# One table set for logarithm and exponential, and two retention gate units placed behind the norm sum

## The chip, the cores and the metric

The kernel runs on one core of a Trainium2 chip. The metric is the device time of one execution in microseconds (us), lower is better. The core has five engines with a queue of instructions each: TensorE (PE, matrix products; its weight loads are shown as PEld), VectorE (DVE), ScalarE (ACT), GpSimd (POOL) and SyncE (SP, which only starts transfers here). They wait for each other through semaphores. ScalarE looks its non-linear functions up in a table set; where a function is not in the loaded set, an ACT_TABLE_LOAD instruction stands before it.

## The reference

Four mixer layers with a feed-forward block behind each work on 512 tokens of width 1024, all in float32. Cut to what the change touches:

```python
# first block: layer 0 latent attention (MLA), layer 1 gated linear recurrence (HGRN)
h = h + rms_norm(mixer(rms_norm(h, g0)), g1)
h = h + rms_norm(sq_relu_mlp(rms_norm(h, g2)), g3)
# HGRN, per head: log_f = log(lb + (1-lb)*sigmoid(f_x)); exp of its cumulated sums; silu(q_x); silu(g_x)
# second block: layer 0 sparse attention (DSA), layer 1 retention
x = x + mixer_2(rms_norm_2(x, g))
x = x + conv_ffn(rms_norm_2(x, g))       # (silu(a) * b) @ w_down
# retention, 4 heads, 256 key and 512 value columns each
ret = rms_norm_2(intra + cross, out_g)   # over the 512 columns of a head
y = ret * silu(g)                        # g: 512 gate columns of the head
out = y @ w_out
```

Each `rms_norm` is x * (mean(x*x) + eps) ** -0.5 * gain.

## The kernel before

**Projections.** Everything is kept transposed: 128 channels on the partitions, 512 tokens along the row. A projection is cut into units, a unit being 128 output columns. SyncE loads a slab of weights (one to four units) into one of two `raw` buffers. GpSimd splits each unit's weights into a high and a low float32r half (`w_hi`, `w_lo`, lines 1176 to 1182; `lo_split` counts finished units), and TensorE makes three products for each chunk of 128 input channels (lines 585 to 587), 24 matmuls for a unit of 8 chunks and 12 for one of 4. Weights and results have a ring of four places: GpSimd may split unit j once unit j-4 is multiplied, and TensorE may begin unit j once VectorE or ScalarE has taken the result of unit j-4 out of its bank (`bank_free`). `unit` does one unit, `units_together` runs several units side by side chunk by chunk, `unit_pair` does two units except their last chunk, then the last chunk of both. A new slab is loaded when its `raw` buffer has been split; `raw_free` gives the count of `lo_split` for which SyncE waits. For the first slab of the second feed-forward block, which runs in a loop, the count is reached when the second of the last four units of the retention's output projection is split.

**Inputs of a projection.** They are split too. ScalarE writes the high half (`a_hi`, line 650, or `g_hi`, line 568), VectorE the low half (`a_lo`, line 663, or `g_lo`, line 572).

**Norms.** ScalarE squares the chunks (line 499), VectorE adds them (line 511), TensorE sums over the partitions with a matrix of ones (line 519), and ScalarE makes the factor in `Norm.root`: a logarithm (line 473), then an exponential of -0.5 times it (line 477). The two functions are looked up in different table sets, so a load stands between them. `AddedNorm.warm` (line 504) runs a one-element logarithm early, so that the logarithm's set is there before the sum. A `LateNorm` stands ahead of a mixer or feed-forward block and is applied to its results, so that units can start before its factor is known; a `PostNorm` stands behind one, in the first block only, and its factor must be there before the residual `hT` can be updated.

**HGRN.** Eight heads. While TensorE works on head i, the gates of head i+1 are prepared on ScalarE (`hg_gates`: SiLU, sigmoid, logarithm, four exponentials) and VectorE; then come head i's norm, the SiLU of the next gate, and `hg_turned`, two copies (lines 1261 and 1263) for which TensorE waits at line 1804.

**Retention.** Four heads, three in a loop and the last one written out with stage `st_ret_end`, whose units are 0 to 3 (values), 4 to 7 (gate) and 8 to 15 (output projection, 4 chunks each). TensorE does the value units, the scores, the four gate units with the remaining scores between them, then scores times values (line 1981) and the two matmuls of the norm sum (lines 549 and 551). VectorE then multiplies each of the four blocks of 128 value columns with gain and factor (line 1680) and with the gate (line 1684), ScalarE rounds it (568) and VectorE makes the low half (572); the output units read these. The second feed-forward block follows directly.

**Keys.** The half-zeroed copies of keys that let two 64-wide heads share one product (`k_rope_odd`, `idx_keys`) are already in this kernel.

Of the kernel before, what the change touches and what calls it, by code (L numbers as in the profile page):

```python
# [182 lines left out]
def program(nc, x, positions, norm_gains, mla_w_in, mla_q_norm, mla_kv_norm, mla_w_uq, mla_w_ukv, mla_w_o, hgrn_w_in,  # L183
# [3 lines left out]
    with ExitStack() as ctx:  # L187
# [52 lines left out]
        qk_gain, act_warm = sb("qk_gain", 1), sb("act_warm", 2)  # L240
# [185 lines left out]

        class Norm:
# [54 lines left out]
        class AddedNorm(Norm):  # L482
# [3 lines left out]
            def __init__(self, chunks, total, tiles=None):  # L486
                super().__init__(chunks)
                self.total, self.running, self.tiles = total, aux[1][:], tiles or sq
# [145 lines left out]
        class LateNorm:  # L634
# [3 lines left out]
            def __init__(self, gain_name, gain_at, total, tiles=None):  # L638
                self.norm = AddedNorm(DC, total, tiles)
                self.high, self.low = shared("late_hi", DC), shared("late_lo", DC)  # L640
                self.gain = (gain_name, gain_at)
# [36 lines left out]
        class PostNorm:  # L678


            def __init__(self, gain_at, total):
                self.norm = AddedNorm(DC, total)
# [126 lines left out]
        pre_mla = LateNorm("norm", 0, tile(F, 12), sq + [tmp[0]] + [tile(F, 8 + k) for k in range(4)])  # L809
# [293 lines left out]
        pre_ret = LateNorm("mix", DC, tile(F, 14))  # L1103
# [12 lines left out]
        ret_o, ret_raw_ready, ret_y = signal("ret_o", RV), signal("ret_raw_ready", RV, credit=1), signal("ret_y", RV)  # L1116
        n_ret = PairedNorm(RET_HEADS, RET_DV, ret_vT[0])
# [70 lines left out]
        def _(act):  # L1188
# [57 lines left out]
            def hg_gates(i):  # L1246
# [4 lines left out]
                act.activation(hg_logf, hg_f, ACT.Ln).then_inc(hg_logf_ready.sem, 1)  # L1251
                act.wait_ge(*hg_d_ready.at(0, i))
# [19 lines left out]
            with act.Fori(0, HG_HEADS - 1) as i:  # L1272
# [3 lines left out]
                hg_silu(3, hg_gate, hg_gate_ready, i + 1)  # L1276
            hg_turned(HG_HEADS - 1)
# [29 lines left out]
            for r, (b, h) in enumerate(REL):  # L1307
# [7 lines left out]
                if r == IDX_HEADS - 1:  # L1315
                    n_key.root(act, users=idx_ready.at(1))
# [7 lines left out]
            act.wait_ge(*r_factors.at(1))  # L1324
            by_block = lambda t, b: t.rearrange("p (c b) -> p c b", b=TB)[:, :, b:b + 1]
# [21 lines left out]
            def ret_head(st, i, h):  # L1347
# [12 lines left out]
                for m in range(RV):  # L1360
                    s_ret.round(act, tile(g_hi, m), m, h)
            with act.Fori(0, RET_HEADS - 1) as i:
                ret_head(st_ret, i, i)
            ret_head(st_ret_end, 0, RET_HEADS - 1)
# [4 lines left out]
        def _(dve):  # L1369
# [281 lines left out]
            def ret_head(st, i, h):  # L1651
# [17 lines left out]
                take(5, ret_gate[1])  # L1669
                decay(2)  # L1670
                take(6, ret_gate[2])
                decay(3)
                take(7, ret_gate[3])
# [23 lines left out]
            with dve.Fori(0, RET_HEADS - 1) as i:  # L1697
                ret_head(st_ret, i, i)
# [339 lines left out]
```

## Time and profile before

| what | us |
|---|---|
| median of 3 runs (lowest, highest) | 2728.09 (2726.54, 2731.78) |
| profiled execution, whole | 2730.05 |
| profiled execution, first to last instruction (span) | 2728.2 |
| PE busy in it | 2608.1 (96%) |
| POOL busy | 1917.2 (70%) |
| DVE busy | 1086.0 (40%) |
| ACT busy | 729.8 (27%) |

A busy PE is modelled: a matmul of 512 columns is shown with 0.39 us, but at full clock the next one starts 0.227 us after it. The shares are averages over very different stages, so the stages have to be looked at one by one.

### The profile page before, as it was taken

To read this page: it belongs to the slowest core of one execution; us is meant where nothing else is said; L and a number is where in the kernel's file an instruction comes from. 1 tells how busy PE (TensorE), PEld (TensorE's weight loads), DVE (VectorE), ACT (ScalarE), POOL (GpSimd) and SP (SyncE) were. 2 spreads that over 40 slices of the span, in tenths; PEclk is the share of its full clock that TensorE was granted. 3 is DMA by queue.
4 is the path that set the end of the run, shared out by engine and by line. 5 is a ranking of instruction groups with operands and counts; after the bars stand their busy time and mean duration, and the time that the engine had idled before them with its cause. 6 is when DMAs were issued, how large, how long until landed. Compare 5 with 4: busy or idle time off the path is not lost.

```text
span 2728.2 us, 33032 instructions
## 1 busy us (share of the span) xinstructions
PE 2608.1 (96%) x11887; PEld 2113.0 (77%) x11887; DVE 1086.0 (40%) x1898; ACT 729.8 (27%) x1181; POOL 1917.2 (70%) x1652
## 2 busy tenths in 40 slices
PE   6998999998998799999898999999999999899999
PEld 5776888876887688888666888888777877688887
DVE  6443211126766241112457452525441441452433
ACT  3443111014555231001455331202122021321211
POOL 5455888886665578888532588887967856788785
PEclk9999999999999899999899999999999999899999
DMA  4121223332221123233210133332312222233232
GB/s 150 51 70 62 93 93 101 99 92 62 63 76 62 51 83 99 92 97 103 62 47 31 47 107 94 93 95 91 108 62 92 77 66 73 78 107 94 93 97 73
DMA packets 285698, 224.27 MB, mean 82 GB/s; under 512 B 14387, under 2 KB 278556, under 8 KB 285468
## 3 DMA queue, kind: packets, MB, share of 16 engines
q1 hardware_dynamic: 285020, 222.47, 26.6%
q8 instruction: 69, 1.13, 0.2%
q10 hardware_dynamic: 576, 0.40, 0.1%
q14 instruction: 33, 0.27, 0.0%
HBM read 220.75 MB, written 2.10 MB: 82 GB/s over the span
## 4 chain that ended last, share of the span: by engine, by line
PE 86%; DVE 6%; issue 3%; ACT 2%; POOL 1%; DVEq 1%; DMA 1%; ACTq 0%; SPq 0%; POOLq 0%
PE proj L585 26%; PE proj L587 26%; PE proj L586 26%; PE aux L1981 1%; DVE top L1599 1%; PE aux L1823 1%; DVEq L1602 1%; PE aux L1958 1%; POOL w_lo L1182 1%; PE aux L452 1%; PE proj L746 1%; PE aux L519 0%; PE aux L805 0%; POOL w_hi L1177 0%; ACT L477 0%
## 5 line engine op out<-in xcount | busy, mean ns | idle before, releaser
L585 PE MATMUL proj<-a_hi,w_hi 128*128 128x512 f32 x2096 | 836.7, 399 | 37.8 <-DVE a_lo L663 30.3
L587 PE MATMUL proj<-a_hi,w_lo 128*128 128x512 f32 x2096 | 821.7, 392 | 0.0
L586 PE MATMUL proj<-a_lo,w_hi 128*128 128x512 f32 x2096 | 821.5, 392 | 0.0
L1176 POOL TENSOR_TENSOR w_hi<-raw,small 128x512 fp32r<-128x512 f32 x374 | 391.8, 1047 | 576.4 <-PE proj L587 552.6
L1177 POOL TENSOR_TENSOR w_hi<-raw,small 128x512 fp32r<-128x512 f32 (+2 forms) x450 | 484.7, 1077 | 177.6 <-PE proj L587 177.4
L1182 POOL TENSOR_TENSOR w_lo<-raw,w_hi 128x512 fp32r<-128x512 f32 (+2 forms) x450 | 590.5, 1312 | 6.0
L1181 POOL TENSOR_TENSOR w_lo<-raw,w_hi 128x512 fp32r<-128x512 f32 x374 | 486.8, 1302 | 29.3
L585 PEld LDWEIGHTS proj<-a_hi,w_hi 128*128 128x128 f32 x2096 | 397.6, 190 | 129.9 <-issue 39.9
L585 PE MATMUL proj<-g_hi,w_hi 128*128 128x512 f32 x1200 | 473.3, 394 | 16.0 <-DVE g_lo L572 9.9
L586 PE MATMUL proj<-g_lo,w_hi 128*128 128x512 f32 x1200 | 469.6, 391 | 0.0
L587 PE MATMUL proj<-g_hi,w_lo 128*128 128x512 f32 x1200 | 469.2, 391 | 0.0
L586 PEld LDWEIGHTS proj<-a_lo,w_hi 128*128 128x128 f32 x2096 | 397.8, 190 | 85.5 <-issue 3.9
L587 PEld LDWEIGHTS proj<-a_hi,w_lo 128*128 128x128 f32 x2096 | 397.0, 189 | 84.6
L585 PEld LDWEIGHTS proj<-g_hi,w_hi 128*128 128x128 f32 x1200 | 226.8, 189 | 68.0 <-issue 12.7
L587 PEld LDWEIGHTS proj<-g_hi,w_lo 128*128 128x128 f32 x1200 | 227.0, 189 | 47.7
L586 PEld LDWEIGHTS proj<-g_lo,w_hi 128*128 128x128 f32 x1200 | 227.1, 189 | 47.5 <-issue 1.0
L864 ACT ACTIVATE aux<-aux 128x512 f32<-128x512 f32 x64 | 37.3, 582 | 486.8 <-DVE aux L885 464.6
L1081 DVE SCALAR_TENSOR_TENSOR F<-aux,cols,F 128x511 f32<-128x511 f32 (+1 forms) x176 | 131.9, 749 | 83.1 <-ACT F L1051 73.0
L1051 ACT ACTIVATE F<-aux,cols 128x512 f32<-128x512 f32 x88 | 68.6, 779 | 225.2 <-DVE aux L1075 224.3
L1075 DVE TENSOR_TENSOR aux<-proj,F 128x512 f32<-128x512 f32 x88 | 61.5, 698 | 167.5 <-PE proj L587 138.8
L898 DVE TENSOR_TENSOR acc<-proj,acc 128x512 f32<-128x512 f32 x48 | 33.2, 692 | 210.1 <-PE proj L587 210.1
L885 DVE SCALAR_TENSOR_TENSOR aux<-proj,F 128x512 f32<-128x512 f32 x48 | 33.6, 699 | 206.4 <-PE proj L587 206.4
(272 smaller groups left out, 2192.4 us busy)
## 6 DMA issues: line engine op xcount, KB each, us to landing
raw<-in_mlp_w SPq DMA_DIRECT2D x64, 1024.0 KB, 5.3
raw<-in_f_w_up SPq DMA_DIRECT2D x88, 512.0 KB, 4.8
raw<-in_b_w_in SPq DMA_DIRECT2D x24, 1024.0 KB, 5.2
raw<-in_hgrn_w_in SPq DMA_DIRECT2D x32, 512.0 KB, 4.9
raw<-in_f_w_down SPq DMA_DIRECT2D x16, 1024.0 KB, 4.9
raw<-in_b_w_out SPq DMA_DIRECT2D x8, 1024.0 KB, 5.0
raw<-in_a_w_in SPq DMA_DIRECT2D x6, 1024.0 KB, 5.2
raw<-in_f_w_down SPq DMA_DIRECT2D x8, 768.0 KB, 4.2
```

The costliest lines, as they stand in the source:

```text
L585: pe.matmul(psum[r][:], w_hi[r][:, w], xh, start=k == 0, stop=False)
L586: pe.matmul(psum[r][:], w_hi[r][:, w], xl, start=False, stop=False)
L587: last = pe.matmul(psum[r][:], w_lo[r][:, w], xh, start=False, stop=k == kc - 1)
L864: act.activation(self.square[j % 2], self.relu[j % 2], ACT.Square).then_inc(self.split.whole.sem, 1)
L885: dve.scalar_tensor_tensor(self.relu[j % 2], bank[:], 0.0, rstd, ALU.max, ALU.mult).then_inc(*taken(self.st, j))
L1051: act.activation(u, self.x[s][j % 2], ACT.Identity, bias=conv_col(l, 3, c), scale=conv_col(l, 2, c)).then_inc(tap2.sem, 1)
L1075: dve.tensor_tensor(x, bank[:], rstd, ALU.mult).then_inc(*taken(st, n))
L1081: dve.scalar_tensor_tensor(u[:, back:T], x[:, 0:T - back], conv_col(l, k, i * DC + first + j + s * FF2C), u[:, back:T], ALU.mult, ALU.add) ...
L1176: pool.tensor_tensor(hi[:, 0:n], src[:, 0:n], nothing.to_broadcast([P, n, P]), ALU.subtract)
L1177: pool.tensor_tensor(hi[:, n:], src[:, n:], nothing.to_broadcast([P, s.kc - n, P]), ALU.subtract).then_inc(hi_split, 1)
L1181: pool.tensor_tensor(lo[:, 0:n], src[:, 0:n], hi[:, 0:n].bitcast(F32), ALU.subtract)
L1182: pool.tensor_tensor(lo[:, n:], src[:, n:], hi[:, n:].bitcast(F32), ALU.subtract).then_inc(lo_split, 1)
```

## The change

1. **Table sets.** `log_and_exp` loads the set that holds both logarithm and exponential, by name. It is called ahead of the norms that follow a SiLU or a sine (`load=True`: the first norm of the kernel, both feed-forward norms and the retention norm of the second block), in HGRN between the logarithm and the exponentials, once behind the HGRN loop, and in each retention head behind the SiLUs of its gate. All other norms go on with the set that is loaded. `warm` and its one-element logarithm are gone. Two places of DSA load the set `natural_log` by name instead.
2. **Two gate units later.** In the last retention head, gate units 6 and 7 stand behind the norm sum on TensorE; ScalarE and VectorE take them, apply SiLU and multiply between the steps of the output blocks (`ret_late_gate`). The remaining scores move ahead of unit 5. The first two output units run as a pair.
3. **Order of first units.** In both feed-forward blocks of the second block and in the retention, the first two units run one after the other, not side by side.

```diff
+        def log_and_exp(act):
+            act.preload_act_table_set("natural_log_exp_and_others")
...
             def square(self, act, src, c):
-                if c == 0 and self.tiles is sq:
-                    self.warm(act)
+                if c == 0 and self.tiles is sq and self.load:
+                    log_and_exp(act)
...
-                if c == self.chunks - 1 and self.tiles is not sq:
-                    self.warm(act)
-            def warm(self, act):
-                act.activation(act_warm[:, self.gbase % 2:self.gbase % 2 + 1], eps, ACT.Ln)
+                if c == self.chunks - 1 and self.tiles is not sq and self.load:
+                    log_and_exp(act)
...
-        pre_mla = LateNorm("norm", 0, tile(F, 12), sq + [tmp[0]] + [tile(F, 8 + k) for k in range(4)])
+        pre_mla = LateNorm("norm", 0, tile(F, 12), sq + [tmp[0]] + [tile(F, 8 + k) for k in range(4)], load=True)
...
-                self.pre = LateNorm("ffn", DC * l, tile(F, 14))
+                self.pre = LateNorm("ffn", DC * l, tile(F, 14), load=True)
...
-                            units_together(pe, st, range(2), DC, a_hi, a_lo, i, self.pre.low.at)
+                            unit(pe, st, 0, DC, a_hi, a_lo, i, ready=self.pre.low.at)
+                            unit(pe, st, 1, DC, a_hi, a_lo, i)
                             self.pre.norm.sum(pe)
...
-        pre_ret = LateNorm("mix", DC, tile(F, 14))
+        pre_ret = LateNorm("mix", DC, tile(F, 14), load=True)
...
                 act.activation(hg_logf, hg_f, ACT.Ln).then_inc(hg_logf_ready.sem, 1)
+                log_and_exp(act)
...
+            log_and_exp(act)
             hg_turned(HG_HEADS - 1)
...
                 if r == IDX_HEADS - 1:
+                    act.preload_act_table_set("natural_log")
                     n_key.root(act, users=idx_ready.at(1))
...
             act.wait_ge(*r_factors.at(1))
+            act.preload_act_table_set("natural_log")
...
-            def ret_head(st, i, h):
+            def ret_head(st, i, h, last):
...
-                for m in range(RV):
+                early = 2 if last else RV
+                for m in range(early):
                     emptied(act, st, 4 + m, i)
                     act.activation(ret_gate[m], ret_gate[m], ACT.Silu)
+                log_and_exp(act)
...
                     s_ret.round(act, tile(g_hi, m), m, h)
+                    if last and 1 <= m < RV - 1:
+                        emptied(act, st, 4 + m + 1, i)
+                        act.activation(ret_gate[m + 1], ret_gate[m + 1], ACT.Silu).then_inc(ret_late_gate.sem, 1)
...
                         dve.wait_ge(*ret_y.at(m, h))
+                        if last and m >= 2:
+                            dve.wait_ge(*ret_late_gate.at(m - 2))
                         s_ret.free(dve, m, h)
...
                         s_ret.rest(dve, tile(g_lo, m - 1), tile(g_hi, m - 1), m - 1, h)
+                    if last and 1 <= m < RV - 1:
+                        take(4 + m + 1, ret_gate[m + 1])
...
-                for m in range(RV):
+                for m in range(2 if last else RV):
                     unit(pe, st, RV + m, DC, a_hi, a_lo, i)
                     if m == 0:
                         turn(RV - 1)
-                    elif m <= 2:
+                        if last:
+                            scores(2)
+                            scores(3)
+                    elif m <= 2 and not last:
                         scores(m + 1)
...
                 n_ret.sum(pe, h)
...
+                if last:
+                    for m in range(2, RV):
+                        unit(pe, st, RV + m, DC, a_hi, a_lo, i)
...
+                if paired:
+                    unit_pair(pe, st, j, RV, g_hi, g_lo, i, lambda k: s_ret.low.at(k, h))
+                for m in range(2 if paired else 0, DC):
+                    unit(pe, st, j + m, RV, g_hi, g_lo, i,
                          ready=(lambda k: s_ret.low.at(k, h)) if m == 0 else None)
```

## Rows read from the trace of the kernel before

**Rows 1.** The page's first part: busy time, share and instructions of each engine

```profile
PE 2608.1 (96%) x11887; PEld 2113.0 (77%) x11887; DVE 1086.0 (40%) x1898; ACT 729.8 (27%) x1181; POOL 1917.2 (70%) x1652
```

**Rows 2.** Stretches: us, busy of PE, PEld, DVE, ACT, POOL, granted clock, DMA share, GB/s

```profile
960.00:1300.00 340.00, 340.00 (x1497) 281.04 (x1496) 76.00 (x115) 52.25 (x86) 281.94 (x248) 1.00 0.29 93
...
1362.00:1366.00 4.00, 4.00 (x9) 2.39 (x9) 0.00 (x0) 2.28 (x3) 2.26 (x2) 0.50 0.56 199
...
2325.00:2330.00 5.00, 4.38 (x9) 2.53 (x9) 4.20 (x7) 1.24 (x2) 0.00 (x0) 0.50 0.00 0
```

**Rows 3.** Waits of PE: us in total, times, longest us

```profile
PE proj L585 <- DVE a_lo L663: 30.3, 4, 9.3
...
PE proj L585 <- DVE g_lo L572: 9.9, 6, 7.7
...
PE proj L585 <- POOL w_lo L1182: 7.9, 3, 4.6
...
PE aux L1804 <- ACT acc L1263: 6.6, 6, 1.2
...
PE aux L452 <- ACT F L444: 3.8, 3, 2.5
```

**Rows 4.** Groups of ACT instructions: busy us, mean ns, idle time before them

```profile
L477 ACT ACT_TABLE_LOAD x28 | 35.9, 1283 | 0.5
...
L473 ACT ACT_TABLE_LOAD x16 | 20.5, 1283 | 16.2 <-PE aux L452 15.3 <-PE aux L551 0.8
```

**Rows 5.** ACT in order of time, at five places: start, us, instruction

```profile
721.84 1.28 ACT L477 ACT_TABLE_LOAD   x1
...
946.43 1.28 ACT L477 ACT_TABLE_LOAD   x1
947.72 0.63 ACT L477 ACTIVATE F<-F 128x512 f32<-128x512 f32 x1
...
1359.38 1.28 ACT L1296 ACT_TABLE_LOAD   x1
...
1456.34 1.28 ACT L1327 ACT_TABLE_LOAD   x1
```

**Rows 6.** PE in order of time, where it waited, and around the last retention head

```profile
662.14 0.38 PE L1783 MATMUL aux<-F 128*128 128x128 f32 x1 [2.90 <-DVE F L1522]
...
729.45 0.39 PE L1804 MATMUL aux<-acc 32*128 32x128 f32 x4 [1.10 <-ACT acc L1263]
...
1361.57 1.19 PE L452 MATMUL aux<-F,ones_half 128*128 128x512 f32 x1 [2.53 <-ACT F L444]
...
2315.97 1.11 PE L551 MATMUL aux<-F,ones 128*128 128x512 f32 x2
2324.74 0.76 PE L585 MATMUL proj<-g_hi,w_hi 128*128 128x512 f32 x1 [7.65 <-DVE g_lo L572]
...
2356.11 0.77 PE L585 MATMUL proj<-a_hi,w_hi 128*128 128x512 f32 x1 [4.61 <-POOL w_lo L1182]
...
2369.16 0.59 PE L519 MATMUL aux<-F,ones 128*128 128x512 f32 x1
```

**Rows 7.** DVE in order of time, behind the last retention norm

```profile
2321.12 0.75 DVE L1680 SCALAR_TENSOR_TENSOR acc<-acc,cols,F 128x512 f32<-128x512 f32 x1 [6.65 <-ACT F L477]
2321.91 0.69 DVE L1684 TENSOR_TENSOR F<-acc,F 128x512 f32<-128x512 f32 x1
```

**Rows 8.** POOL in order of time, output units 12 and 13, then the feed-forward's first

```profile
2331.70 1.04 POOL L1177 TENSOR_TENSOR w_hi<-raw,small 128x512 fp32r<-128x512 f32 x1 [22.59 <-PE proj L587]
...
2335.25 1.04 POOL L1177 TENSOR_TENSOR w_hi<-raw,small 128x512 fp32r<-128x512 f32 x1 [1.15 <-PE proj L587]
...
2345.12 1.04 POOL L1176 TENSOR_TENSOR w_hi<-raw,small 128x512 fp32r<-128x512 f32 x1 [1.68 <-DMA raw<-in_f_w_up]
...
2350.06 1.49 POOL L1176 TENSOR_TENSOR w_hi<-raw,small 128x512 fp32r<-128x512 f32 x1
```

**Rows 9.** SP in order of time: the load for the feed-forward block

```profile
2338.16 41.33 SPq L1149 DMA_DIRECT2D raw<-in_f_w_up  x10
```

More of the change, by code:

```diff
@@ L482, in program, with __init__ @@
         class AddedNorm(Norm):
[L486 removed]
+            def __init__(self, chunks, total, tiles=None, load=False):
                 super().__init__(chunks)
[L488 removed]
+                self.total, self.running, self.tiles, self.load = total, aux[1][:], tiles or sq, load
             def square(self, act, src, c):
                 n = len(self.tiles)
[L493 to L494 removed]
+                if c == 0 and self.tiles is sq and self.load:
+                    log_and_exp(act)
                 if self.base > 0 and c == 0:
@@ L634, in program, with __init__ @@
         class LateNorm:
-            def __init__(self, gain_name, gain_at, total, tiles=None):
-                self.norm = AddedNorm(DC, total, tiles)
+            def __init__(self, gain_name, gain_at, total, tiles=None, load=False):
+                self.norm = AddedNorm(DC, total, tiles, load)
                 self.high, self.low = shared("late_hi", DC), shared("late_lo", DC)
@@ L678, in program, with __init__ @@
         class PostNorm:
-            def __init__(self, gain_at, total):
-                self.norm = AddedNorm(DC, total)
+            def __init__(self, gain_at, total, load=False):
+                self.norm = AddedNorm(DC, total, load=load)
                 self.scaled, self.added = shared("post_scaled", DC), shared("post_added", DC)
@@ L1649, in ret_rotate, with ret_head @@
                     dve.tensor_tensor(dst[1], tmp[1], dst[1], ALU.add).then_inc(ret_qk_ready.sem, 1)
-            def ret_head(st, i, h):
+            def ret_head(st, i, h, last):
                 def take(j, dst):
@@ L1668, in ret_head @@
                 take(4, ret_gate[0])
[L1669 to L1673, printed above, removed]
+                if last:
+                    decay(2)
+                    decay(3)
+                    take(5, ret_gate[1])
+                else:
+                    take(5, ret_gate[1])
+                    decay(2)
+                    take(6, ret_gate[2])
+                    decay(3)
+                    take(7, ret_gate[3])
                 dve.wait_ge(*ret_v_turned.at(2, h))
@@ L1936, in _ @@
             ffn[0].pe(pe)
-            units_together(pe, st_ret_qk, range(2), DC, a_hi, a_lo, 0, pre_ret.low.at)
+            unit(pe, st_ret_qk, 0, DC, a_hi, a_lo, ready=pre_ret.low.at)
+            unit(pe, st_ret_qk, 1, DC, a_hi, a_lo)
             pre_ret.norm.sum(pe)
@@ L1942, in _, with ret_head @@
                 unit(pe, st_ret_qk, j, DC, a_hi, a_lo)
-            def ret_head(st, i, h):
+            def ret_head(st, i, h, last):
                 def turn(m):
@@ L1957, in scores @@
                     for c in range(2):
-                        last = pe.matmul(aux[b % 2][:, 0:w], ret_k[c][:, b * P:b * P + P], ret_q[c][:, b * P:T],
+                        done = pe.matmul(aux[b % 2][:, 0:w], ret_k[c][:, b * P:b * P + P], ret_q[c][:, b * P:T],
                                          start=c == 0, stop=c == 1)
-                    last.then_inc(ret_scores.sem, 1)
+                    done.then_inc(ret_scores.sem, 1)
                 for m in range(RV):
@@ L1980, in ret_head, with ret_out @@
                         e = b * RET_DV + m * P
-                        last = pe.matmul(aux[2 + m % 2][:, b * P:T], ret_vtok[:, e:e + P], ret_s[b][:, 0:T - b * P],
+                        done = pe.matmul(aux[2 + m % 2][:, b * P:T], ret_vtok[:, e:e + P], ret_s[b][:, 0:T - b * P],
                                          start=b == 0, stop=b == TB - 1, skip_group_check=True)
-                    last.then_inc(ret_o.sem, 1)
+                    done.then_inc(ret_o.sem, 1)
                 n_ret.sum(pe, h)
-            def ret_out(st, j, i, h):
-                for m in range(DC):
-                    unit(pe, st, j + m, RET_DV // P, g_hi, g_lo, i,
+                if last:
+                    for m in range(2, RV):
+                        unit(pe, st, RV + m, DC, a_hi, a_lo, i)
+            def ret_out(st, j, i, h, paired=False):
+                if paired:
+                    unit_pair(pe, st, j, RV, g_hi, g_lo, i, lambda k: s_ret.low.at(k, h))
+                for m in range(2 if paired else 0, DC):
+                    unit(pe, st, j + m, RV, g_hi, g_lo, i,
                          ready=(lambda k: s_ret.low.at(k, h)) if m == 0 else None)
             with pe.Fori(0, RET_HEADS - 1) as i:
-                ret_head(st_ret, i, i)
+                ret_head(st_ret, i, i, False)
                 for j in range(8, 12):
```

15 lines of the change are left out of this document (8 added, 7 removed).

## The prediction

> **What bounds the kernel now.** I read the page's first part, then the granted clock and busy times by stretch, the waits of TensorE, the load groups of ScalarE, and last the timeline around each wait. TensorE is busy 96% of the span [rows 1]. In a long stretch of MLP blocks it never pauses: 1497 matmuls in 340 us at full clock, so 0.227 us each, 5.45 us for a unit of 24 and 2.72 us for one of 12 [rows 2]. There nothing on another engine can gain or lose time. What is left are TensorE's waits, and their list is short: 30.3 us for the low half of an input in 4 places, 9.9 us for `g_lo` in 6, 7.9 us for split weights in 3, 6.6 us for HGRN's copies in 6, 3.8 us for a square in 3 [rows 3]. So each part of the change is worth what it takes out of one of these waits, plus what the clock does: behind some waits it is granted at 0.50, which of its two levels is 1.2 GHz [rows 2].
>
> **Part 1, the table loads.** A load takes 1.283 us. 28 stand between a norm's logarithm and exponential and 16 before the logarithm [rows 4]. Counting through the diff, 108 loads become 60, but most stand where TensorE has other work (every `LateNorm`: units run while its factor is made). Those on TensorE's path:
>
> - The four `PostNorm`s: the chain is sum, logarithm, load, exponential, update of `hT`, `a_hi`, `a_lo`, and TensorE idles all through (the 30.3 us). The logarithm's load was already early; the one before the exponential goes [rows 3, 5]: 4 x 1.28 = 5.1. Late next is the same chain without the load, so all of it counts.
> - HGRN's loop: TensorE waits 1.10 for the copies at line 1804 [rows 6], six times, 6.6 in sum [rows 3]. ScalarE reaches them by norm, rounding and gate SiLU, and the load between logarithm and exponential lies in that chain [rows 5]. Without it the copies are 1.28 earlier, a little more than the wait. The shown waits start from a modelled matmul end that lies some 0.16 behind the next possible issue (0.39 shown against 0.227). So between 6.6 and 6 x 1.28 = 7.7; I take 7.2, as wait plus overlap just fits into the load. The new load behind the gates' logarithm replaces an automatic one.
> - HGRN's entry: TensorE waits 2.90 for the first head's gates, behind the norm's factor [rows 6]; that chain loses one load: 1.3. The loads for SiLU, sigmoid and logarithm stay.
> - Short waits for `g_lo`: apart from the 7.65 [rows 6], the 9.9 holds 2.2 in five waits [rows 3]. Three of them, 1.6 together, lie in MLA and in HGRN's last head, behind norms that lose two loads or one, more than each wait: 1.6 (bounds 0 and 2.2). The extra load behind HGRN's loop comes while TensorE runs two early output units; without that cover it would cost 1.28.
> - DSA: TensorE waits 2.53 for a square that stands behind a load and a small exponential [rows 5, 6]: 1.3. Behind this wait the clock is at 0.50 for 4 us in which 9 matmuls run [rows 2], 2.0 us more than 9 x 0.227. Half the wait may or may not keep the clock up: I take half, 1.0 (bounds 0 and 2.0). Against it: the load at line 1327 started directly behind a copy [rows 5], and the named load now stands behind two semaphore waits, with the logarithms and the query copies queued behind it and TensorE waiting for those. It can be late by 0 to 1.28; I take 0.5, since VectorE's selection ends at about the same time. Sum 1.8.
>
> In the retention loop the new load stands before the first square. TensorE has scores times values, then four more units there, so I cost it at nothing; if the first copy came too late for its third group of matmuls, it would be up to 1.28 a head.
>
> **A page against the row.** The load's neighbour starts 0.01 us behind it: 946.43 plus 1.28, then 947.72 [rows 5]. The Trainium skill, "ScalarE: Activation LUTs", section "What ACT_TABLE_LOAD costs", gives 1283 ns for the load and about 1380 ns more for a drain. By it an estimate of the four `PostNorm`s would be 10.6 instead of 5.1. The drain is not in this row, so the load alone counts.
>
> **Part 3, order of first units.** With `units_together` TensorE needs two split units, now one. At the retention's start that is a short wait for weights; the 7.9 us in 3 waits [rows 3] is 4.6 at the second feed-forward (counted below) and 3.3 elsewhere, most of it in HGRN's output projection, which doesn't change. I take 0.5 (bounds 0 and 3.3). The first feed-forward starts without a wait: 0.
>
> **Part 2, the two gate units.** Clock zero is the end of the norm sum, 2315.97 + 1.11 = 2317.08 in the trace before [rows 6]. Before, the first low half lets TensorE go at 7.65, at half clock at first [rows 2]; then come 8 output units; then 4.61 of waiting for weights; and at 52.1 (2369.16) the two first feed-forward units are done [rows 6]. Their pure work is 8 x 2.72 + 2 x 5.45 = 32.7, so 19.4 us are waits and slow clock. The gate units cost 10.9 ahead of zero, so the old stretch is 63.0.
>
> After, from the same zero, which now comes 10.9 earlier:
> - Factor: 2321.12 was 4.04 behind zero [rows 7]; without two loads 1.5. First low half 3.6 later (2324.74 - 2321.12): 5.1.
> - Second: VectorE must take unit 6, done at 5.45, then 0.7 for each of take, multiply, product and low half [rows 7], SiLU 0.6 between: 8.3 to 9. ScalarE has to load the SiLU set here, but while it waits for VectorE.
> - Third and fourth: unit 7 is done at 10.9, taken at 11.7, multiply, product: 13.1, low half 13.8, last rounding and low half 14.5. These waits sit in VectorE's queue; behind them are only the output blocks, for which TensorE waits.
> - TensorE: gate units to 10.9, two chunks of unit 8 to 12.3, waits to 13.9, then 18 matmuls of the pair to 18.0, units 10 to 15 to 34.3.
> - GpSimd: before, unit 12 was begun at 2331.70, unit 13 waited 1.15, and the feed-forward load started at 2338.16, 6.46 later, 5.3 without the wait; the weights were used from 2345.12, 6.96 behind the load's start; unit 16 took 4.94, unit 17 with hand-over 6.05 [rows 6, 8, 9]. After: unit 8 is done at 17.3, unit 12 begins at 17.7, the load starts at 23.0, unit 16 is split from 30.0 to 35.0, unit 17 is ready at 41.0.
> - TensorE: unit 16 from 35.2 to 40.7 (part 3: it needn't wait for unit 17), unit 17 from 41.0 to 46.5. Its input is complete some 3 us behind 34.3, earlier than chunk 7 needs it.
>
> 63.0 - 46.5 = 16.5. Bounds: only the idle time at the norm goes, 7.65 and two small waits, 8.3; everything goes, 19.4.
>
> **Sum.** 5.1 + 7.2 + 1.3 + 1.6 + 1.8 + 0.5 + 16.5 = 34.0. The profiled execution took 2730.05, 1.96 above the median of 2728.09; by it 2696.0, by the median 2694.1. I give 2694.
>
> **The rivals.**
> - *The weights give the gain back*: GpSimd or the load for the feed-forward keeps its old time, so the output units run earlier but TensorE waits longer at 2356 [rows 6]. For it: the load starts only behind unit 13's split [rows 8, 9]. Against: unit 13 itself hangs on TensorE's unit 9, which moves. Gain 8.3 there, 25.8 in all: 2702.
> - *The named loads change nothing*: automatic loads stay wherever they were. Then parts 2 and 3 alone remain, 17.0: 2711. The trace before has two loads in each norm although one set could serve both [rows 4], so placement doesn't look for it. The Trainium skill, "ScalarE activation tables: per-element evaluation and per-set limits", section "Table sets in the compiler and the runtime", says that loads are placed by the longest run per block. By that rule the pair would have been one load already; the trace disagrees.
> - *The clock gains more*: with shorter waits it stays up behind DSA's wait and at HGRN's output too, 5 us more than I took: 2689.
> - *Slower*: the new order leaves TensorE at 0.50 from the last retention head on. Rows show 0.50 beside waits and 1.00 over the long stretch without one [rows 2], which speaks against it. Each us at half clock costs half a us of work, so it decides from 2 x 34 = 68 us; lasting 100 us it gives -34 + 50: 2744.
> - *No change* needs most of the waits to be taken over by others, such as VectorE in HGRN and GpSimd in the retention: 2727.
>
> **How the numbers follow.** Forecast 0.70 (its own range 2686 to 2702), weights 0.12, named loads 0.07, clock 0.06, no change 0.03, slower 0.02. The range reaches from the clock case with every term at its upper bound, 2684, to a point between the weights and the named loads, 2707. Within 0.2% (5.5 us) is what a measurement of this kernel can't tell from no change. Faster by more: 0.70 + 0.12 + 0.07 + 0.06 = 0.95; same 0.03; slower 0.02.
>
> **What would show it.** In the profile after: some 60 loads, none at line 477 outside DSA's two named places; the waits for `a_lo` at about 25 in 4; no wait at 1804 for the copies; two gate units directly behind the norm sum, then less than 3 us of waiting and a clock of 1.00; the wait for `w_lo` before the second feed-forward at about 1; from norm sum to that block's own sum 46.5 us. The forecast is wrong if the first low half is late because VectorE stands at a gate unit, if the feed-forward load doesn't move with unit 13, or if the copies at 1804 wait for something else than the norm.

## The result and the profile after

| | median us | lowest to highest | runs |
|---|---|---|---|
| before | 2728.11 | 2726.54 to 2731.78 | 4 |
| after | 2690.86 | 2688.88 to 2692.70 | 4 |

After takes 0.986 of before, 95% interval 0.9845 to 0.9875: faster by 37.25 us, where 34.0 were forecast. The profiled execution after took 2692.35 (span 2690.6). Its page begins with

```profile
PE 2594.2 (96%) x11887; PEld 2106.2 (78%) x11887; DVE 1090.8 (41%) x1898; ACT 666.6 (25%) x1121; POOL 1922.3 (71%) x1652
```

against [rows 1]. TensorE's idle time fell from 2728.2 - 2608.1 = 120.1 to 2690.6 - 2594.2 = 96.4, so by 23.7. The same 11887 matmuls are shown busy for 13.9 us less. That second part is the clock: a matmul at half clock is drawn longer. More than a third of the gain of the traces, 13.9 of 37.6 us, comes this way.

ScalarE's table loads, by group (the sites with one load each left out):

```profile
L429 ACT ACT_TABLE_LOAD x17 | 21.8, 1283 | 0.2
L1247 ACT ACT_TABLE_LOAD x17 | 21.8, 1283 | 0.3
L1254 ACT ACT_TABLE_LOAD x8 | 10.3, 1283 | 0.1
...
L1362 ACT ACT_TABLE_LOAD x4 | 5.1, 1283 | 0.1
```

Of the two big groups of [rows 4], 28 and 16 loads, one load is left; all sites together hold 60 loads. Line 429 is the new named load. TensorE's waits that answer to [rows 3]:

```profile
PE proj L586 <- DVE a_lo L664: 26.5, 4, 9.1
...
PE aux L1952 <- ACT F L1346: 7.3, 2, 5.2
...
PE proj L586 <- POOL w_lo L1185: 3.4, 2, 2.8
...
PE proj L586 <- DVE g_lo L573: 2.6, 1, 2.6
...
PE aux L456 <- ACT F L448: 2.6, 3, 1.2
```

The wait for HGRN's copies (6.6 in 6) is no longer in the list. `g_lo` fell from 9.9 to 2.6, the weights from 7.9 to 3.4, and the wait for a square in DSA went from 2.53 to 1.25. The second row grew, from 6.6 in 2 places; it stands in DSA and comes back below. TensorE at the end of the retention, from the norm's second sum to the sum of the second feed-forward's own norm:

```profile
2281.73 1.11 PE L552 MATMUL aux<-F,ones 128*128 128x512 f32 x2
...
2297.76 0.79 PE L586 MATMUL proj<-g_hi,w_hi 128*128 128x512 f32 x1 [2.63 <-DVE g_lo L573]
...
2320.48 0.50 PE L586 MATMUL proj<-a_hi,w_hi 128*128 128x512 f32 x1 [0.65 <-POOL w_lo L1185]
...
2331.53 1.02 PE L520 MATMUL aux<-F,ones 128*128 128x512 f32 x2
```

With the forecast's zero, the end of the norm sum at 2281.73 + 1.11 = 2282.84, the stretch is 48.7 us. Before, it was 63.0 with the gate units' 10.9 [rows 6]; the forecast was 46.5.

Two traces are compared below by the start of the same matmul in each. The start-up alone (waits for the first tables and the input) differs by about 1 us between executions of one kernel, so single differences under 1 us say little. The clock behind a wait can differ by more with the same code, as shown further below; so the table says where the time went in these two traces, and not what each step is worth in every execution.

| step of the forecast | forecast | by the two traces |
|---|---|---|
| four `PostNorm`s | 5.1 | 5.1 |
| HGRN's loop | 7.2 | 6.8 |
| HGRN's entry | 1.3 | 1.1 |
| short `g_lo` waits | 1.6 | 6.1 (MLA 1.0, HGRN's last head 3.3, its output units 1.8) |
| DSA | 1.8 | 2.9 (2.55 - 0.68 + 1.05) |
| start of the retention | 0.5 | 0.8 |
| norm sum to second feed-forward | 16.5 | 14.4 |
| start-up | 0 | 0.4 |
| sum | 34.0 | 37.6 |

### The profile page after: what moved, and what is told of

It is laid out like the page before. It is cut to its first block, busy times and chain, and to the rows that moved or that the text cites. A ratio compares the mean times of both kernels' runs of the same rounds, so it can differ in the third digit from the quotient of the medians.

```text
span 2690.6 us, 32976 instructions
## 1 busy us (share of the span) xinstructions
PE 2594.2 (96%) x11887; PEld 2106.2 (78%) x11887; DVE 1090.8 (41%) x1898; ACT 666.6 (25%) x1121; POOL 1922.3 (71%) x1652
## 4 chain that ended last, share of the span: by engine, by line
PE 92%; DVE 4%; issue 2%; ACT 1%; DMA 0%; POOL 0%; ACTq 0%; DVEq 0%; SPq 0%; POOLq 0%
PE proj L586 28%; PE proj L587 27%; PE proj L588 27%; PE aux L2006 1%; PE aux L806 1%; PE aux L1844 1%; PE aux L1980 1%; PE aux L1923 1%; PE aux L456 1%; PE proj L747 1%; PE aux L1928 1%; PE aux L520 0%; DVE F L694 0%; PE proj L1783 0%; PE proj L1784 0%
## 5 line engine op out<-in xcount | busy, mean ns | idle before, releaser
L586 PE MATMUL proj<-a_hi,w_hi 128*128 128x512 f32 x2096 | 834.5, 398 | 28.6 <-DVE a_lo L664 26.5
L865 ACT ACTIVATE aux<-aux 128x512 f32<-128x512 f32 x64 | 37.3, 582 | 489.3 <-DVE aux L886 464.6
```

The costliest lines, as they stand in the source:

```text
L586: pe.matmul(psum[r][:], w_hi[r][:, w], xh, start=k == 0, stop=False)
L865: act.activation(self.square[j % 2], self.relu[j % 2], ACT.Square).then_inc(self.split.whole.sem, 1)
```

## Experiments

### Each part alone

Part 1 alone is the kernel after with `ret_head(..., False)` everywhere, output units not paired, and `units_together` at both places. Part 2 alone has the old tables and `units_together`. Part 3 alone is:

```diff
-units_together(pe, st, range(2), DC, a_hi, a_lo, i, self.pre.low.at)
+unit(pe, st, 0, DC, a_hi, a_lo, i, ready=self.pre.low.at)
+unit(pe, st, 1, DC, a_hi, a_lo, i)
```

and the same two lines for `st_ret_qk`. Then the kernel after without part 3, and the kernel after without part 2.

Expected of part 1 alone:

> Part 1 alone on the kernel before. The forecast's terms give 5.1 (PostNorms) + 7.2 (HGRN's loop) + 1.3 (its entry) + 1.6 (short waits) + 1.8 (DSA) = 17.0, and one load less behind the retention's last norm sum, where TensorE waited 7.65 us: 1.3 to 2.6 more there, unless the weights take it back at the second feed-forward. So 2710, and 2711 if they do. If the two traces' alignment is right instead, the parts outside the retention's end are worth 23.3 us with part 3's small share in them, so 2705. If the named loads changed nothing, it would stay at 2728.

Of part 2 alone:

> Part 2 alone: the two gate units behind the norm sum, with the old table loads and with the first feed-forward units still side by side. The forecast for parts 2 and 3 together was 16.5 from the norm sum on. Side by side, TensorE can begin the pair of units only when unit 17 is split, so about 5.4 us of that should be missing: 11 us, so 2717. The factor is two loads (2.6 us) later behind the norm sum, but hidden behind the two gate units (10.9 us). If the old loads do sit on the path, 8 us, 2720. If the weights take all of it back: 0 to 3 us.

Of part 3 alone:

> Part 3 alone: first units one after the other. At the second feed-forward TensorE waited 4.61 us for two split units; it would need only unit 16 first, and unit 17 is ready about 6 us after it, while unit 16's matmuls take 5.45. So about 4 of the 4.61 us go, and up to 0.5 at the retention's start: 4.5 us, 2723.6. The rival, that the input's last chunk (not the weights) is what comes late there, gives 0.5 us or less, 2727.6, which could not be told from no change.

Of after without part 3:

> The kernel after without part 3 (first units of the second and later blocks side by side again). In the trace after, unit 17 is ready about 5.3 us behind unit 16. With both needed at the start, the forecast's reckoning makes it slower than the kernel after by 5 us, 2696. If part 3 is worth only its wait in the kernel before (4.0), 2695; if the weights were no limit after part 2, the difference is below 1 us, 2691.

Of after without part 2:

> The kernel after without part 2 (all four gate units of the last head ahead of its norm sum, output units not paired). By the runs so far, from the norm sum to the second feed-forward's own sum (10.9 us added where the gate units lie ahead of it) the tables alone took 59.5 us, tables with gates late 55.4, all three 48.7, old tables with part 3 alone 54.7. If the parts add up, this one takes 59.5 - 6.7 = 52.8, so 4.1 us more than after: 2695. If part 3 is worth more here, as it was on the old kernel (8.3), 51.2 and 2693.4. By the forecast, in which the gate units were most of 16.5 us, it would be about 10 us slower than after, 2701.

Measured (medians of 4 to 12 executions; "stretch" is the retention's end as above, from the norm sum to the feed-forward's own sum, with 10.9 added where the gate units lie ahead of the sum):

| parts | us | ratio to before, 95% | stretch | wait for weights in it |
|---|---|---|---|---|
| none (before) | 2728.1 | 1 | 63.0 | 4.61 |
| 1 | 2701.7 | 0.9906 (0.9894 to 0.9919) | 59.5 | 4.57 |
| 2 | 2721.5 | 0.9979 (0.9970 to 0.9988) | 56.7 | 5.96 |
| 3 | 2718.1 | 0.9964 (0.9953 to 0.9975) | 54.7 | 0 |
| 1, 2 | 2698.5 | 0.9890 (0.9876 to 0.9905) | 55.4 | 5.94 |
| 1, 3 | 2694.9 | 0.9872 (0.9857 to 0.9887) | 53.4 | 0 |
| 1, 2, 3 (after) | 2690.9 | 0.9860 (0.9845 to 0.9875) | 48.7 | 0.65 |

The kernels were run in jobs, each with before beside them. Before had a median of 2727.5 in the job of parts 1, 2, 3 and of 1 with 2, and of 2731.9 in the job of parts 1 with 3; gains of a part alone are taken against 2727.5. The stretches come from one execution each, and not always a typical one: the traces of parts 2 and 3 alone are of the slowest execution of their kernel (2728.1 and 2724.7), the trace of parts 1 and 3 is of the fastest (2692.1 of 2692.1 to 2700.6).

What follows:

- Part 1 is the largest, 25.8 us of the 37.3. Named loads do move the automatic ones, so the forecast's second rival is out. By the forecast's terms I had expected 2710, by the two traces 2705; it came out at 2701.7. Ahead of the last retention head its trace agrees with after's within 1.8 us, so the terms up to there are too small in it as they are in after, mostly by the clock in HGRN; and the stretch gave 3.5 where I had expected 1.3 to 2.6.
- The gate units alone are worth 6.0, and on top of the tables 3.2 (2701.7 - 2698.5). I had expected 11. My step was wrong there: it took the whole idle time at the norm as gain and let GpSimd follow. Parts 1 and 2 together show where it goes:

```profile
2297.47 0.50 PE L586 MATMUL proj<-g_hi,w_hi 128*128 128x512 f32 x1 [2.63 <-DVE g_lo L573]
...
2324.11 0.76 PE L586 MATMUL proj<-a_hi,w_hi 128*128 128x512 f32 x1 [5.94 <-POOL w_lo L1184]
```

The wait at the norm is short (2.63 instead of 5.09 with part 1 alone), and the wait for the feed-forward's two split units is 1.4 longer than with part 1 alone (5.94 and 4.57). The stretch is 4.1 shorter; what the waits don't explain is the clock behind the norm's wait, 0.50 for 4 us with part 1 alone and 1.00 here. So the weights do give gain back while part 3 is missing, as that rival has it, but 1.4 us and not all of it.

- With the tables and part 3 in place, the gate units take the median from 2694.9 to 2690.9, as expected (2695), but the two ratios' intervals overlap, and the two traces as a whole are only 0.3 us apart (spans of 2690.3 and 2690.6): the one without part 2 was 5 us ahead before the last retention head, in code that is the same in both. The stretch, 53.4 against 48.7, is the better evidence.
- Part 3 is worth 9.4 alone (the stretch says 8.3), twice the 4.5 that I expected of it, and 7.6 on top of the others (2698.5 - 2690.9; I had expected 5). It takes away the wait, and with it the slow clock behind the wait. The same 4 us by the clock of each trace, before and then with part 3 alone (busy us and counts of PE, PEld, DVE, ACT, POOL, granted clock, DMA share, GB/s):

```profile
2356.00:2360.00 4.00, 3.89 (x9) 3.14 (x10) 0.00 (x0) 0.00 (x0) 3.92 (x4) 0.50 0.67 193
```

```profile
2356.00:2360.00 4.00, 4.00 (x19) 3.33 (x18) 1.10 (x2) 0.00 (x0) 3.92 (x4) 1.00 0.17 44
```

Nine matmuls against 19: 0.50 is 1.2 GHz, 1.00 is 2.4 GHz. The trace before draws the two units as 2369.16 - 2356.11 = 13.05 us where 10.9 is their pure time [rows 6]. So 4.61 + 2.15 = 6.8 hang on this one wait. My expectation of part 3 had counted about 4 of the wait and nothing for the clock.

### What a load costs

```diff
+act.preload_act_table_set("natural_log")
+log_and_exp(act)
 act.activation(to, log_ms, ACT.Exp, scale=-0.5)
```

in the four `PostNorm`s of the kernel after, with `natural_log` loaded and then the common set again.

> The kernel after with two more named table loads between logarithm and exponential in each of the four PostNorms (eight loads in all, no other difference). By the rows a load costs its 1.283 us and no more: 8 x 1.28 = 10.3 us slower than the kernel after, 2701. If a drain of about 1.38 us stood behind each load, as the Trainium skill, ScalarE: Activation LUTs, section What ACT_TABLE_LOAD costs, states, it would be 8 x 2.66 = 21.3 us, 2712. If loads of a set that is there already, or names, had no effect, 2691.

Measured: 2703.6 us, 12.8 more than after. The wait for `a_lo`:

```profile
PE proj L589 <- DVE a_lo L667: 35.8, 4, 11.0
```

It rose from 26.5 by 9.3 us for eight loads. Two of the four waits, the second and the fourth, grew by 2.57 each, which is 2 x 1.285. So a load costs its own duration on this path. The first grew by 2.25 and the third by 1.91. The spans of the two traces are 11.1 apart. The 1.8 beyond the waits is a sum over places where the granted clock differs with the same code, among them 1.8 lost in HGRN's last head and 1.5 behind DSA, 1.9 won at the retention's end (see the end of this section). By the drain that the Trainium skill, "ScalarE: Activation LUTs", section "What ACT_TABLE_LOAD costs", adds, it would have been 21.3; this trace disagrees.

**Where two of the removed loads went.** The loads that the change removed show the same pattern. From before to after, the second and fourth waits shrank by 1.28, the first by 0.95 and the third by 0.29. In the third, VectorE begins its first multiply 1.27 earlier behind the sum, and meets more of GpSimd's splits. VectorE and GpSimd in the trace after, behind HGRN:

```profile
928.55 2.76 DVE L694 SCALAR_TENSOR_TENSOR F<-acc,cols,F 128x512 f32<-128x512 f32 x2 [2.79 <-ACT F L481]
931.23 1.75 DVE L698 TENSOR_TENSOR hT<-hT,F 128x512 f32<-128x512 f32 x1
933.01 1.64 DVE L694 SCALAR_TENSOR_TENSOR F<-acc,cols,F 128x512 f32<-128x512 f32 x1
...
932.39 1.71 POOL L1185 TENSOR_TENSOR w_lo<-raw,w_hi 128x512 fp32r<-128x512 f32 x1
```

The last of these multiplies took 0.75 before, when GpSimd had ended 0.59 us ahead of it, and takes 1.64 now. From VectorE's first multiply to TensorE's start it is 6.52 us before and 7.51 after: 0.99 of the 1.28 is given back. In the second and fourth places GpSimd is idle and nothing is given back. No run moved GpSimd's work here; that it is the cause is read from the traces, and from the experiment on the same pair of engines further below.

### DSA's second load ahead of its waits

```diff
+act.preload_act_table_set("natural_log")
 act.wait_ge(sq_used.sem, n_dq.base + n_dq.chunks)
 act.wait_ge(*r_factors.at(1))
-act.preload_act_table_set("natural_log")
```

> The kernel after with DSA's second named load ahead of the two semaphore waits that it now stands behind. In the comparison of the traces, the stretch with that load is 0.68 us longer than before. My theory: the load lies exposed between the waits and the logarithms, and ahead of them it is hidden: 0.7 us faster than after, up to 1.28. The rival, that VectorE's selection ends last there and not ScalarE: 0. Either is near the limit of the times; the wait of TensorE behind it (5.21 us after, 4.57 before) decides.

Measured: 2689.3 (2688.6 to 2690.0), ratio 0.9852 (0.9836 to 0.9869), which overlaps with after's. ScalarE after, then with the edit:

```profile
1433.64 0.58 ACT L1327 COPY acc<-proj 128x512 f32<-128x512 f32 x1
1434.87 1.28 ACT L1331 ACT_TABLE_LOAD   x1 [0.66 <-PE aux L468]
```

```profile
1431.60 0.58 ACT L1327 COPY acc<-proj 128x512 f32<-128x512 f32 x1
1432.20 1.28 ACT L1329 ACT_TABLE_LOAD   x1
```

The load starts directly behind the copy again, and TensorE's longest wait in DSA is back from 5.2 to 4.6. So the mechanism is right and worth 0.64 at this wait; the times can't confirm it.

The trace as a whole doesn't win it. Some 55 us later TensorE has a wait of 1.92 us for `g_lo`. The 4 us behind it, first in the kernel with GpSimd's splits later (next part), whose DSA load is late, then with this edit:

```profile
1493.00:1497.00 4.00, 4.00 (x18) 3.31 (x18) 0.00 (x0) 0.00 (x0) 0.00 (x0) 1.00 0.00 0
```

```profile
1493.00:1497.00 4.00, 4.00 (x11) 3.20 (x12) 0.00 (x0) 0.00 (x0) 0.00 (x0) 0.60 0.00 0
```

18 matmuls against 11. From this wait to the next norm sum it takes 54.5 us in ten kernels, and 56.0 in the three with DSA's load early and in the one with eight more loads. So the edit wins 0.64 at the wait and, in each of its three traces, 1.5 us are lost behind the next one. Why the clock falls there is not shown.

### Why VectorE's products were slow

In the trace after, VectorE's third and fourth products stand at

```profile
2290.03 1.66 DVE L1703 TENSOR_TENSOR F<-acc,F 128x512 f32<-128x512 f32 x1
...
2295.47 1.63 DVE L1703 TENSOR_TENSOR F<-acc,F 128x512 f32<-128x512 f32 x1
```

and GpSimd splits weights at

```profile
2289.53 1.62 POOL L1185 TENSOR_TENSOR w_lo<-raw,w_hi 128x512 fp32r<-128x512 f32 x1
...
2294.97 1.59 POOL L1185 TENSOR_TENSOR w_lo<-raw,w_hi 128x512 fp32r<-128x512 f32 x1
```

GpSimd's subtractions end at 2291.15 and 2296.56, and each product ends 0.54 behind them, at 2291.69 and 2297.10. The forecast had them at 0.69 [rows 7]. The multiplies ahead of them took 1.02 instead of 0.75 as well. GpSimd restarts exactly when a gate unit is done, because that frees the place for the next split, and the same event sets VectorE going. The edit holds the two splits back:

```diff
 pool.wait_ge(unit_done, st.done(j - RING, i))
+if st is st_ret_end and j in (10, 11):
+    pool.wait_ge(*s_ret.low.at({10: 1, 11: 3}[j], RET_HEADS - 1))
```

> The kernel after with GpSimd's splits of units 10 and 11 of the last retention head held back until low halves 1 and 3 are made. In the trace after, VectorE's third and fourth products took 1.66 and 1.63 us instead of 0.69, while GpSimd split these units. My theory is that the two slow each other down: the products should take 0.69 again, TensorE's wait 2.63 become about 1.5, and the time 1.2 us shorter, 2.9 if the clock then stays up (it was 0.66 for some 4 us behind the wait). If the products are long for another reason (they come directly behind a multiply that rewrites their operand), nothing changes in them, and the time is the same or, with units 10 to 13 later, longer.

Measured: 2688.0 (2687.1 to 2688.7), ratio 0.9849 (0.9833 to 0.9866). VectorE and TensorE in its trace:

```profile
2287.19 0.69 DVE L1705 TENSOR_TENSOR F<-acc,F 128x512 f32<-128x512 f32 x1 [0.17 <-DVE acc L1699]
...
2292.56 0.69 DVE L1705 TENSOR_TENSOR F<-acc,F 128x512 f32<-128x512 f32 x1
```

```profile
2293.90 0.51 PE L586 MATMUL proj<-g_hi,w_hi 128*128 128x512 f32 x1 [1.47 <-DVE g_lo L573]
...
2315.21 0.50 PE L586 MATMUL proj<-a_hi,w_hi 128*128 128x512 f32 x1 [0.57 <-POOL w_lo L1187]
...
2326.25 1.02 PE L520 MATMUL aux<-F,ones 128*128 128x512 f32 x2
```

The products are 0.69 again (and the multiplies 0.74), the wait 1.47 instead of 2.63. The clock stays at 1.00 behind it, where after had 0.66 for 4 us:

```profile
2298.00:2302.00 4.00, 4.00 (x13) 3.17 (x14) 0.48 (x1) 0.00 (x0) 0.00 (x0) 0.66 0.00 0
```

```profile
2293.00:2298.00 5.00, 4.10 (x18) 3.37 (x19) 1.86 (x4) 0.62 (x1) 2.54 (x3) 1.00 0.00 0
```

The stretch is 46.1 us, 2.6 less than after and 0.4 from the forecast's 46.5. Only 1.2 of this is the edit's for certain, the shorter wait. The clock can stay up without it: in the kernel with DSA's load early the products are as slow (1.66 and 1.64), and behind the same wait TensorE goes at

```profile
2296.71 0.50 PE L586 MATMUL proj<-g_hi,w_hi 128*128 128x512 f32 x1 [2.64 <-DVE g_lo L573]
...
2297.00:2301.00 4.00, 4.00 (x19) 3.25 (x19) 0.97 (x2) 0.00 (x0) 0.43 (x1) 1.00 0.00 0
```

with a stretch of 47.5 (the second line is the 4 us behind the wait, by engine as above). With eight more loads it is 46.8. So the slow products are shown as the cause of 1.2 us of what the forecast's step missed. Behind the wait of 2.6 us the clock was low in both traces of after and up in three other kernels; behind the wait of 1.47 it was up in all four kernels that have it. The times leave the edit open: 2688.0 and after's 2690.9 have intervals that overlap.

The Trainium skill, "SBUF — State Buffer", section "SBUF: two separate sides", has a shared port pair, by which a VectorE instruction with two SBUF operands and a GpSimd instruction that reads SBUF lock each other out for whole instructions. The ends 0.54 behind GpSimd's agree with a lock rather than with both running slower.

### Is it the edit or the hour, and a better version

Three further edits: the feed-forward's first load is meant to be issued behind unit 11's split, whose buffer it takes (`raw_free` uses the four units of the slab before in the first turn); the output units are not paired; DSA's load is early as above. First the splits, the load and DSA's load together (the load's edit took no effect, see below):

> Splits later and DSA's load early together, and the first load for the second feed-forward issued behind unit 11's split instead of unit 13's (its buffer is free by then; 2308.38 in the trace after, some 11 us earlier here). TensorE's 0.65 us wait for unit 16 goes. Sum by my theory 0.7 + 1.2 + 0.65 = 2.6 us faster than after, 4.3 if the clock stays up as well: 2687 to 2688. If unit 17's split stays the limit of the feed-forward's start (GpSimd's splits in order, not the load), about 1.3 us: 2689.5.

Then after once more, beside two versions without the pair:

> The kernel after itself, without an edit, beside the others of this job: 2690.9 by its first four runs. The run with the splits later took 2688.0 in another job. If that was a property of the chip or the hour and not of the edit, this one comes at 2688 too; if the edit is worth the 2.6 us that its trace shows, it stays above 2690.

> Splits of units 10 and 11 later, and the output units one after the other instead of units 8 and 9 paired. In the trace with the splits later, low half 3 is ready 0.7 us behind low half 2, for which TensorE waits, so unit 8 can finish without a second wait and 2 us earlier than in the pair. GpSimd's unit 12 hangs on unit 8 and everything behind it moves by up to 2 us; TensorE's wait of 0.57 for unit 16 goes. My theory: 0.6 us faster than the splits alone, 2687.4. The rival, that the pair is needed to keep TensorE in work while VectorE makes the last low halves, gives one more wait of 0.3 to 0.7 us and a low clock behind it: 2689.

> The last one, and also the first load of the second feed-forward behind unit 11's split, and DSA's second named load ahead of its waits. The three edits together were no faster than the splits alone (2689.2 against 2688.0), though TensorE's wait behind DSA's load was 0.64 shorter. With unit 12 two us earlier the load would be the next limit, so it may count now: 2686.5. If GpSimd's chain of splits alone sets the feed-forward's start, no difference from the last one: 2687.4.

| kernel | us | lowest to highest | ratio to before, 95% | stretch |
|---|---|---|---|---|
| splits later | 2688.0 | 2687.1 to 2688.7 | 0.9849 (0.9833 to 0.9866) | 46.1 |
| splits later, both loads early | 2689.2 | 2688.0 to 2691.0 | 0.9854 (0.9837 to 0.9870) | 46.0 |
| after again | 2691.5 | 2690.2 to 2693.2 | 0.9851 (0.9836 to 0.9866) | 48.5 |
| splits later, not paired | 2687.5 | 2687.4 to 2689.4 | 0.9838 (0.9824 to 0.9851) | 45.6 |
| the same, both loads early | 2687.3 | 2686.6 to 2689.2 | 0.9840 (0.9827 to 0.9854) | 45.7 |

The last three rows come from one job, in which before itself had a median of 2731.9; so their ratios are compared among themselves. After again stays above all ten runs of the two unpaired versions beside it, by 4 us at the median. In the traces the stretch is 2.9 shorter: 1.2 by the norm's wait, 0.5 by the wait for weights, the rest by the clock. Without the pair the wait for weights (0.57) is gone and the stretch 0.5 shorter, as expected. These two versions are the fastest of the study, 0.15% below after, and can't be told from each other.

**The early load of the feed-forward was not tested.** The edit asks `if st is st_ffn[1][0]`, but the entries of `st_ffn[1]` are tuples of a stage and two numbers, so this is never true and the load stays where it was. The trace with all three edits has it directly behind unit 13's split:

```profile
2303.68 1.30 POOL L1190 TENSOR_TENSOR w_lo<-raw,w_hi 128x512 fp32r<-128x512 f32 x1
...
2305.16 1.53 SPq L1152 DMA_DIRECT2D raw<-in_f_w_up  x2
```

The split ends at 2304.98, 0.18 ahead of the load, and the distance is the same within 0.01 in the kernels without the edit. From the norm sum's end to the load it is 23.0 us with the splits later (with and without the edit) and 22.4 without the pair (again both). So the second row of the table is the first with DSA's load early, and the last is the one above it with DSA's load early. The expected 2.6 us from all three did not come: 2689.2 is 1.2 above the splits alone, and the two traces differ by 0.6 won at DSA's wait and 1.4 lost behind the next, as above. The last pair differs by 0.2. What an earlier feed-forward load is worth stays open.

### A clock that differs with the same code

In the third `PostNorm`, behind HGRN, the time from the start of the `a_lo` wait to the next norm sum fell into two groups over ten kernels with the new tables (the one with more loads aside): 33.8 us in after, after again, and the splits without the pair, 32.2 us in the seven others. Ahead of this place these ten kernels differ in nothing. After again, then splits later:

```profile
937.03 0.76 PE L586 MATMUL proj<-a_hi,w_hi 128*128 128x512 f32 x1 [9.06 <-DVE a_lo L664]
...
961.81 1.02 PE L520 MATMUL aux<-F,ones 128*128 128x512 f32 x2
```

```profile
936.51 0.77 PE L586 MATMUL proj<-a_hi,w_hi 128*128 128x512 f32 x1 [9.02 <-DVE a_lo L664]
...
959.69 1.02 PE L520 MATMUL aux<-F,ones 128*128 128x512 f32 x2
```

After the same wait it is 24.78 against 23.18. The windows behind it have the granted clock at 0.50 and then 0.72 in the one (9 and 14 matmuls in 4 us), at 0.58 and 1.00 in the other (10 and 19). The same happens in HGRN's last head. From the wait at the square of the scores (0.80 at line 1837) to the norm sum it is 7.1 us in the three kernels with the old tables, 5.2 in ten with the new ones. But it is 7.0 in the kernel with more loads, whose HGRN code is that of after. After, then that kernel:

```profile
885.00:890.00 5.00, 4.22 (x22) 3.05 (x21) 0.00 (x0) 0.69 (x2) 0.00 (x0) 0.76 0.00 0
```

```profile
895.00:900.00 5.00, 4.22 (x12) 2.88 (x12) 0.00 (x0) 1.26 (x2) 0.00 (x0) 0.50 0.00 0
```

So 1.9 of the 3.3 us that the last head gained is a clock that came out better, not a load that was on the path. What decides it is not settled. With the 1.5 us behind DSA and the 1.2 to 1.9 at the retention's end, these are four places where the same code behind the same wait takes one of two times; together they are some 6 us, as much as part 2 gave alone.

## Why the prediction was right, and where it was off

The time is 3.1 us below the forecast of 2694.0 and inside its own range (2686 to 2702); the rival "the clock gains more" had 2689 and is nearer, 1.9 away. By its steps:

- **`PostNorm`s**: 5.1 of 5.1, by luck. "The same chain without the load, so all of it counts" was wrong in two of four places: the waits shrank by 0.95, 1.28, 0.29 and 1.28, 3.8 in sum, because VectorE met GpSimd's splits in the first and third, as the traces show. The other 1.3 is clock, and in seven other kernels with the new tables the third place alone gained 1.6 more of it. That a load costs 1.28 on this path stands, shown by the added loads.
- **HGRN's loop and entry**: right in both. The copies' wait is gone, 6.8 of 7.2, and 1.1 of 1.3.
- **Short `g_lo` waits**: the step that was most off, 6.1 instead of 1.6. Its waits were sized rightly (0.78, 0.30 and 0.54; the last lies at HGRN's output units and not in its last head), but not the clock at them: 1.9 us of the last head is clock, and so is at least part of the 1.8 at the output units. The forecast credited the clock only in DSA.
- **DSA**: the wait fell from 2.53 to 1.25 as forecast, and the named load behind the waits cost 0.64 where I took 0.5. Wait and clock together gave 2.55, more than the 2.3 that I took; another 1.05 between DSA's output and the first feed-forward is assigned to nothing.
- **Norm sum to second feed-forward**: 14.4 instead of 16.5. The term "0.7 for each of take, multiply, product and low half" was mis-sized: two products took 1.6 and their multiplies 1.0, because GpSimd works at the same moment. The wait was 2.63 instead of 1.6, the clock fell for 4 us, and units 12 to 16 came later. With the splits moved, the forecast's own number came out (46.1 for 46.5), 1.2 of it by the shorter wait and the rest by a clock that also stays up without the move in other kernels.
- **The split between parts 2 and 3** was not forecast by number, but its reasoning put the gain on the gate units. The runs put it the other way: on top of the others, 4.7 of the stretch for them, 6.7 for the order of the first units.
- **The rivals**: "the clock gains more" gave 2689 and is, in part, what happened together with the forecast: more clock outside the retention, less gain in it. "The weights give the gain back" happens in part without part 3 (1.4 us). The named loads did act, and nothing was slower.

The two large errors, +4.5 at the short `g_lo` waits and -2.1 in the retention, have opposite signs, and inside the `PostNorm`s a wait that shrank too little and a better clock cancel. So the causes of the gain are right and their sum is close partly by luck.

## What to carry to other kernels

A short wait of TensorE is worth more than its length when the clock is granted at 0.50 behind it: here 4.61 us of waiting for weights gave 6.8, so read the granted clock behind each wait before pricing it. But one trace does not settle it: the same wait had either clock in other kernels. An edit of 1 us can be judged by its wait, hardly by its time. Before relying on the duration of a VectorE operation in a new place, look at what GpSimd does at that moment, above all when one event releases both. And read in the trace that an edit of order took effect before concluding that it is worth nothing. Where two units of work need two prepared inputs at once, starting with the one that is ready can be worth more than finding cover for the wait.

## What the hardware showed unexpectedly

- VectorE's product of 128x512 took 1.63 to 1.66 us beside a split on GpSimd, and 0.69 when the split was moved away.
- Two table loads in a row added 2.57 us to each of two waits, and nothing beyond their own 1.283 each. In two other places removing a load of 1.283 shortened the wait by 0.95 and 0.29 alone, with VectorE's operations longer beside GpSimd's.
- The same code behind the same wait of 9 us took 1.6 us more or less by the granted clock, in three kernels of ten the slow way. Behind a wait of 1.92 us it was 1.5 us more in the three kernels with an edit some 55 us ahead of it and in the one with more loads, and in none of the ten others.
